# Output projection as seven quadrant products, and the stores of the residual stream ahead of fifteen expert chunks

## What is computed

```python
merged = jax.nn.sigmoid(gate_r) * y_ret + jax.nn.sigmoid(gate_m) * y_m
x = x + merged @ w_out                     # (512, 1024) @ (1024, 1024)
h = rms_norm(x, norm_ffn_w)
# router: group, then two experts of it for every token
y_e = (silu(h @ w_gate[e]) * (h @ w_up[e])) @ w_down[e]      # 32 experts, 1024 x 512 x 1024
x = x + sum over the token's two experts of weight * y_e
out = rms_norm(x, norm_final_w)
```

## Time and profile before

| | |
|---|---|
| median of three runs | 1023.38 us |
| the profiled execution | 1022.9 us |
| its span, first to last instruction | 1021.0 us |
| granted clock of TensorE, mean | 0.996 |
| TensorE matmuls, busy | 996.3 us (98%) |
| VectorE, ScalarE, GpSimd, busy | 500.1, 323.9, 120.8 us |
| moved by DMA | 269.3 MB, mean 264 GB/s |

### The profile page before, as it was taken

How to read it: one execution, slowest core, us unless ns; L and a number is a source line. 1 busy time by engine, 2 the same in 40 slices (tenths; PEclk the granted TensorE clock), 3 DMA queues, 4 the chain that set the end, 5 groups by cost and what they waited for, 6 DMA issues and landing times.

```text
span 1021.0 us, 13126 instructions
## 1 busy us (share of the span) xinstructions
PE 996.3 (98%) x4917; PEld 644.4 (63%) x4917; DVE 500.1 (49%) x810; ACT 323.9 (32%) x531; POOL 120.8 (12%) x152
## 2 busy tenths in 40 slices
PE   8999999999999999999998999999999999999896
PEld 7888788889889988888885333333333333333332
DVE  6268646597778677735525123333223233332235
ACT  6344535586556557622213100000000000000012
POOL 0683077000000000000000000000000000000000
PEclk9999999999999999999999999999999999999999
DMA  9223231344334525162988899999999999999993
GB/s 331 83 83 126 92 114 21 83 125 145 66 91 113 185 42 205 43 213 90 422 307 357 348 420 420 420 420 420 420 420 420 421 420 420 420 421 421 421 414 146
DMA packets 63125, 269.28 MB, mean 264 GB/s; under 512 B 9488, under 2 KB 9680, under 8 KB 38360
## 3 DMA queue, kind: packets, MB, share of 16 engines
q1 hardware_dynamic: 57464, 257.32, 63.6%
q0 software_dynamic: 5344, 11.02, 4.9%
q10 hardware_dynamic: 256, 0.10, 0.0%
HBM read 268.41 MB, written 4.20 MB: 267 GB/s over the span
## 4 chain that ended last, share of the span: by engine, by line
PE 72%; SPq 17%; DVE 5%; DMA 3%; ACT 2%; issue 1%; DVEq 0%; ACTq 0%
PE pj L674 23%; PE pj L854 18%; PE pj L956 12%; SPq L575 11%; PE pj L982 6%; SPq L572 6%; PE cb L631 3%; DMA raw_moe<-in_w_up_dram 3%; PE cb L992 2%; PE cb L993 1%; DVE mkT L1758 1%; DVE wl L1494 1%; PE cb L723 1%; PE cb L695 1%; ACT wh L1136 1%
## 5 line engine op out<-in xcount | busy, mean ns | idle before, releaser
L956 PE MATMUL pj<-raw_moe,xT 128*64 128x512 f32 x1016 | 227.6, 595 | 4.2 <-DMA raw_moe<-in_w_up_dram 2.4
L1494 DVE TENSOR_TENSOR wl<-raw_mix,wh 128x1024 fp32r<-128x1024 f32 x116 | 146.2, 1262 | 130.9 <-ACT wh L1136 130.6
L1970 DVE TENSOR_TENSOR x<-x,cb 128x512 f32<-128x512 f32 x120 | 77.0, 683 | 190.2 <-PE cb L993 190.2
L956 PEld LDWEIGHTS pj<-raw_moe,xT 128*64 128x64 f32 x1016 | 72.1, 137 | 140.8 <-issue 140.8
L1136 ACT ACTIVATE wh<-raw_mix 128x1024 fp32r<-128x1024 f32 x116 | 122.4, 1057 | 111.4 <-PE pj L674 68.5
L982 PE MATMUL pj<-raw_moe,hf 128*64 128x512 f32 x512 | 116.7, 598 | 1.6 <-ACT hf L1440 1.6
L982 PEld LDWEIGHTS pj<-raw_moe,hf 128*64 128x64 f32 x512 | 34.6, 136 | 67.2 <-issue 67.0
L1445 ACT ACTIVATE yh<-pj,now 128x512 fp32r<-128x512 f32 x32 | 20.4, 683 | 157.6 <-PE cb L993 143.6
L1440 ACT ACTIVATE hf<-cb 128x512 f32<-128x512 f32 x16 | 9.6, 598 | 146.3 <-PE cb L631 146.3
L992 PE MATMUL cb<-yh,hot 128*128 128x512 f32 x124 | 55.2, 445 | 0.0
L674 PE MATMUL pj<-wh,hTh 128*128 128x512 f32 x128 | 50.8, 397 | 1.7 <-DVE hTl L1525 0.7
(11 more groups left out here) (397 smaller groups left out, 1858.5 us busy)
## 6 DMA issues: line engine op xcount, KB each, us to landing
raw_moe<-in_w_gate_dram SPq DMA_DIRECT2D x64, 1024.0 KB, 26.7
raw_moe<-in_w_down_dram SPq DMA_DIRECT2D x64, 1024.0 KB, 26.7
raw_moe<-in_w_up_dram SPq DMA_DIRECT2D x63, 1024.0 KB, 26.0
raw_mix<-in_w_in_dram SPq DMA_DIRECT2D x31, 1024.0 KB, 5.3
raw_mix<-in_w_in_dram POOLq DMA_DIRECT2D x10, 512.0 KB, 5.8
raw_mix<-in_w_ret_branch_dram SPq DMA_DIRECT2D x4, 1024.0 KB, 5.8
raw_mix<-in_w_mlstm_branch_dram SPq DMA_DIRECT2D x4, 1024.0 KB, 5.5
raw_mix<-in_w_out_dram SPq DMA_DIRECT2D x4, 1024.0 KB, 5.1
```

What stands on the lines that cost most here:

```text
L956: mm = nc.tensor.matmul(pj[a * CAP:(a + 1) * CAP, up, :], xT[:, 4 * half + k, a * CAP:(a + 1) * CAP], weights_of(m + a)[:, k, :], start=ha ...
L1494: V.tensor_tensor(wl[:, q % RING, :, :], entry_source(q), wh[:, q % RING, :, :].bitcast(F32), ALU.subtract).then_inc(wl_ok, 1)
L1970: V.tensor_tensor(part, part, cb[:, 2 + g % 2, :], ALU.add).then_inc(c_add, 1)
```

## The change

The output projection is no longer two blocks but seven products of quadrants (`U_11` to `U_T4`), each in two halves `s` of 128 rows, with 14 ring entries in place of 16. The activation quadrants and their sums and differences are made by DVE (`out_part_sum`, `out_part_tail`), ACT (`out_part_head`) and POOL (`combined`, two more calls). Four quadrants of `w_out` are loaded into expert places by SP (`out_load`), three more into the ring of raw weights, and POOL issues 14 accumulating DMAs of 512 KB that make the sums of weights (`out_sums`). The results are gathered into `x2` by DVE: seven kinds of adds and subtractions of 128x512, two tiles each. Tiles 0 and 1 of `x2` are ready after the fifth product, tiles 2 and 3 after the two halves of the last one (`tile_ready`). Turning tiles 0 and 1 and the first half of the logits now stand between the products, the work on the router's weights too.

On SP only chunks 21, 13, 14, 7, 8 and 0 are left in front of the stores; the four stores follow, each behind the wait for its tile, and then fifteen chunks. Four places of `raw_moe` are exchanged. The diff, cut to its core:

```diff
-BLOCKS = 22
+BLOCKS = 20
...
-ENTRIES = 4 * (BLOCKS - 2 * len(FAST)) + FAST_ENTRIES
+OUT0 = 4 * (BLOCKS - 2 * len(FAST)) + FAST_ENTRIES
+ENTRIES = OUT0 + 2 * PRODUCTS
...
+        mrgTf = at("mrgTf", 48, [P, KD, T])
+        e5h = at("e5h", 0, [P, 4, 256], F32R)
+        e5f = at("e5f", 4, [P, 4, 256])
+        e5l = at("e5l", 24, [P, 4, 256], F32R)
+        s2h = at("s2h", 8, [P, 4, 256], F32R)
+        s2f = at("s2f", 12, [P, 4, 256])
+        s2l = at("s2l", 12, [P, 4, 256], F32R)
+        e3h = at("e3h", 16, [P, 4, 256], F32R)
+        e3f = at("e3f", 20, [P, 4, 256])
+        e3l = at("e3l", 20, [P, 4, 256], F32R)
+        t1c = at("t1c", 28, [P, 2, 512])
...
-                   enumerate([64, 72, 0, 8, 16, 24, 80, 88, 144.0625, 152.0625, 104, 120, TOP, TOP + 8, 32, 40, 48, 56, 96, 112, 194.5625, 186.0625])]
+                   enumerate([64, 72, 0, 8, 16, 24, 80, 88, 144.0625, 152.0625, 96, 112, TOP, TOP + 8, 32, 40, 48, 56, 104, 120, 194.5625, 186.0625])]
...
+        out_slot = {U_11: 12, U_T1: 13, U_T2: 0, U_T4: 1}
+        out_sums = (U_T1, U_T2, U_T2, U_T4, U_T4, U_T4, U_T3)
+        def out_place(u):
+            return raw_moe[out_slot[u]] if u in out_slot else raw_mix[slot_of(2 * B_WO + (U_T3, U_22, U_21).index(u))]
+        def out_full(u, s):
+            if u in (U_T1, U_22):
+                return tr_ps, 2 * KD + (2 if u == U_22 else 0) + s + 1
+            if u == U_21:
+                return full[2 + s], full_of(2 + s, B_WM + 1) + 1
+            return full[s], full_of(s, B_WM + 1) + (U_11, U_T2, U_T3, U_T4).index(u) + 1
+        def out_free(s, n):
+            return free[s], free_of(s, B_WM + 1) + n
+        def tile_ready(t):
+            return out_free(t % 2, 2 + t // 2 * 2)
+        def stream_bank(t, half):
+            return cb[:, 2 * t + half, :] if t < 2 else pj[:, 6 - 2 * t + half, :]
...
+            def out_load(u, c):
+                sp.dma_start(out_place(u)[:, :, :], w_out[0][0:512, 512 * c:512 * (c + 1)].rearrange("(k p) n -> p k n", p=P))\
+                    .then_inc(moe_in[out_slot[u]], 16)
+            for n in range(2 * B_WR, 2 * B_WO + 3):
+                if n == 2 * B_WR + 3:
+                    sp.wait_ge(full[1], full_fast(len(FAST) - 1, U_T2, 1))
+                    out_load(U_11, 0)
+                    out_load(U_T1, 1)
+                if n == 2 * B_WR + 4:
+                    sp.wait_ge(tr_ps, KD)
+                    out_load(U_T2, 1)
+                    out_load(U_T4, 1)
...
-            moe_chunk(13, 0, False)
-            moe_chunk(14, 0, False)
             sp.wait_ge(it_ok, 1)
             moe_chunk(21, 0, False)
-            sp.wait_ge(tr_ps, KD)
-            moe_chunk(0, 0, False)
-            moe_chunk(1, 0, False)
-            sp.wait_ge(full[3], full_of(3, B_WO - 1))
-            for m in (2, 3, 5, 6):
-                moe_chunk(m, 0, False)
-            sp.wait_ge(mgl_ok, KD)
+            sp.wait_ge(wl_ok, out_entry(U_11, 1) + 1)
+            moe_chunk(13, 0, False)
+            sp.wait_ge(wl_ok, out_entry(U_T1, 1) + 1)
+            moe_chunk(14, 0, False)
+            sp.wait_ge(mgl_ok, 7)
             moe_chunk(7, 0, False)
             moe_chunk(8, 0, False)
-            sp.wait_ge(wl_ok, ENTRIES)
-            moe_chunk(9, 0, False)
-            moe_chunk(10, 0, False)
-            sp.wait_ge(*entry_used(ENTRIES - 3))
-            for m in (11, 12, 15, 17):
-                moe_chunk(m, 0, False)
+            sp.wait_ge(wl_ok, out_entry(U_T2, 1) + 1)
+            moe_chunk(0, 0, False)
             for t in range(TT):
-                sp.wait_ge(free[t], free_of(t, BLOCKS - 1))
+                sp.wait_ge(*tile_ready(t))
                 sp.dma_start(x_dram[t * P:(t + 1) * P, :], x2[:, t, :]).then_inc(st_in, 16)
-            for m in (16, 18, 19, 20):
+            for m in (1, 2, 3, 5, 6, 9, 10, 11, 12, 15, 17, 16, 18, 19, 20):
...
-            pe.wait_ge(tr_l, 2 * KD)
-            for t in range(TT):
-                turn_stream(t)
-            pe.wait_ge(wrt_ok, 1)
-            logits(0)
+            out_parts = ((mrgTh[:, low, lower], mrgTl[:, low, lower]), (mrgTh[:, high, lower], mrgTl[:, high, lower]), (e5h, e5l), (e3h, e3l), (s2h, s2l),
+                         (mrgTh[:, low, upper], mrgTl[:, low, upper]), (mrgTh[:, high, upper], mrgTl[:, high, upper]))
+            def out_half(u, s):
+                if u == U_11:
+                    pe.wait_ge(*out_free(s, 0))
+                if u == U_21:
+                    pe.wait_ge(*out_free(2 + s, 0))
+                if u == U_22:
+                    pe.wait_ge(tr_h, 2 * KD + s + 1)
+                if u in (U_T2, U_T3, U_T4):
+                    pe.wait_ge(*out_free(s, (U_T2, U_T3, U_T4).index(u) + 1))
+                if s == 0:
+                    pe.wait_ge(mgl_ok, (1, 3, 4, 5, 6, 2, 7)[u])
+                ah, al = out_parts[u]
+                o = cb[:, s, :] if u in (U_T1, U_22) else pj[:, 2 + s, :] if u == U_21 else pj[:, s, :]
+                rows = slice(s * P, (s + 1) * P)
+                for v in range(2):
+                    q = out_entry(u, v)
+                    if s == 0:
+                        pe.wait_ge(wl_ok, q + 1)
+                    for kk in range(2):
+                        k = 2 * v + kk
+                        ops = ((ah[:, k, rows], wh[:, q % RING, kk, :]), (al[:, k, rows], wh[:, q % RING, kk, :]),
+                               (ah[:, k, rows], wl[:, q % RING, kk, :]))
+                        for n, (lhsT, rhs) in enumerate(ops):
+                            m = nc.tensor.matmul(o, lhsT, rhs, start=u in (U_11, U_21, U_T1) and k == 0 and n == 0,
+                                                 stop=k == 3 and n == 2, skip_group_check=True)
+                    if v == 1:
+                        m.then_inc(out_full(u, s)[0], 1)
+                    elif s == 1:
+                        m.then_inc(pair_used, 1)
+            for u in range(PRODUCTS):
+                for s in range(2):
+                    out_half(u, s)
+                    if u == U_T3:
+                        turn_stream(s)
+                    if u == U_T4 and s == 0:
+                        pe.wait_ge(wrt_ok, 1)
+                        logits(0)
+            turn_stream(2)
+            logit_rows(0)
+            turn_stream(3)
             logits(1)
...
+            def out_part_head(n):
+                if n in (0, 2, 6):
+                    act.wait_ge(mg_ok, 4 if n == 0 else KD)
+                if n == 0:
+                    act.wait_ge(*entry_used(entry(B_WM, 0) - 1))
+                if n in (1, 3):
+                    act.wait_ge(sum_ok, 6 * len(FAST) + (1 if n == 1 else 2))
+                if n in (4, 5):
+                    act.wait_ge(rope_ok, 2 * TT + 4 + (2 if n == 4 else 1))
+                lower, upper = slice(0, 256), slice(256, 512)
+                dst, src = ((mrgTh[:, 0:4, lower], mrg[:, 0:4, lower]), (mrgTh[:, 0:4, upper], mrgTf[:, 0:4, upper]), (mrgTh[:, 4:8, lower], mrg[:, 4:8, lower]),
+                            (e5h, e5f), (e3h, e3f), (s2h, s2f), (mrgTh[:, 4:8, upper], mrg[:, 4:8, upper]))[n]
+                nc.scalar.activation(dst[:, :, :], src[:, :, :], ACT.Copy).then_inc(mgh_ok, 1)
...
+            for x in range(2 * PRODUCTS):
+                if x == 0:
+                    out_part_head(2)
+                if x in (2 * U_T1 + 1, 2 * U_T1 + 2):
+                    out_copy(x - 2 * U_T1 - 1)
+                if OUT0 + x + LEAD < ENTRIES:
+                    mix_head(OUT0 + x + LEAD)
+                if x == 0:
+                    out_part_head(3)
+                if x in (3, 4, 5):
+                    out_part_head(x + 1)
+                if x == 2 * U_T3 + 1:
+                    square(0)
+                    stream_copy(0)
+                if x == 2 * U_T4:
+                    square(1)
+                    stream_copy(1)
...
+            def out_part_sum(n):
+                dve.wait_ge(mg_ok, 4 if n == 0 else KD)
+                lower, upper = slice(0, 256), slice(256, 512)
+                dst, one, two = ((mrgTf[:, 0:4, upper], mrg[:, 0:4, lower], mrg[:, 0:4, upper]), (e5f, mrg[:, 0:4, upper], mrg[:, 4:8, upper]))[n]
+                V.tensor_tensor(dst[:, :, :], one, two, ALU.subtract).then_inc(sum_ok, 1)
...
+                if x in (9, 10):
+                    upper_right_last(x - 9)
+                if x in (11, 12):
+                    lower_right_last(x - 11)
+                    stream_turned(x - 11)
+                if x == 13:
+                    lower_left(0)
+                if OUT0 + x + LEAD < ENTRIES:
+                    mix_tail(OUT0 + x + LEAD)
+                if x == 0:
+                    out_part_tail(2)
+                    out_part_tail(3)
+                if x in (1, 2):
+                    first_sum(x - 1)
+                if x in (3, 4):
+                    out_part_tail(x + 1)
+                if x == 5:
+                    second_sum(0)
+                    second_sum(1)
```

(35 more changed lines are left out.)

137 lines of the change are left out of this document (85 added, 52 removed).

## The result

The changed kernel takes 1052.16 us (median of four runs, 1051.13 to 1055.64) against 1022.89 for the kernel before: a ratio of 1.0291, with a 95% interval of 1.0265 to 1.0317. It is slower by 29 us, where 17 were forecast, and outside the range.

The account below looks back on a forecast made before the run. The weight stream was taken to bound the kernel: starting full 29.1 us earlier but with 19.1 MB (45.5 us) more left, +16.4 on 1022.9 gives 1039.3, plus 0.5 for the median 1039.8 us; range 1033 to 1048.

Parts of the forecast that it names:

- What bounds the kernel: Expert stage: nearly balanced, DMA the limit at the end; with weights always there it would end 3.7 us sooner.
- TensorE's saving: Output projection: 168 matmuls instead of 192, 38.1 us instead of 43.5, 5.4 us less.
- the first stall: Projection's second product: waits for the third part's tail, ready at 497.9, after the first product ends at 496.5: 1.4 us.
- DVE's release of a bank: Projection's sixth product: waits 0.3 to 1.3 us for it, 5.8 if all eight POOL operations take 1.81.
- The moved loads: SP queue: fifteen loads now behind tile 3's wait, eleven fewer under the projection; end of the stream moves by +16.4 us.
- 25 us of cover: Accumulating loads: fourteenth ends near 488, needed about 513 for the eleventh weight head; at 8 us each, 514, just late.
- two chained sums on POOL from 494.5: Projection's fourth part: 5.8 to 14.5 us of sums, 9.8 by the median, covered before its product at 508.8.
- the stalls inside the projection: TensorE's new waits in the output projection: together 1.7 to 2.7 us, bounds 0 and 7.2.
- The chain's pace: Fourteen accumulating loads of 512 KB, each after the one before landed: 6.15 us apiece, 86 us; a loaded queue 8 us.
- Rival B: Projection itself stalls: accumulate chain past 513 us, branch chunk after 467, or POOL sums late; 1047 to 1054; chance 0.13.
- The guest wait: First up product: guest chunk, last in line, lands at 580.5; TensorE stalls some 14 us, overlapping the stream's lateness.
- The branch landing beside an accumulate: Branch chunk at 454.3: up to 13 us later, at 467, if queues take turns; again just in time.

Follow-up runs that it names:

- e2: Changed kernel with the two activation sums made by DVE and none on GpSimd, accumulating loads untouched: 1041.03 us, ratio 1.0156 to 1.0250.
- e3: Kernel before, with only the order of SP's first loads changed as in the change (six, the stores, fifteen others): 1040.65 us, ratio 1.0158 to 1.0187.
- e5: e2 with each expert load issued as its place comes free, between and ahead of the stores: 1032.3 us, ratio 1.0052 to 1.0117.
- e4: Changed kernel with the guest chunk and token row issued after nine of the fifteen loads: 1054.52 us, ratio 1.0278 to 1.0329.
- e6: e2 with the guest chunk and row indices issued after nine of the fifteen loads: 1041.48 us, ratio 1.0155 to 1.0265.
- e1: Changed kernel with GpSimd's two activation sums ahead of the last two accumulating loads, not behind all fourteen: 1046.1 us, ratio 1.0208 to 1.0242.
- e12: e9 with only eight expert loads ahead of the last two stores, and the last three held until the first gather landed: 1034.33 us.
- e9: e5 with the expert loads that began at 508 held until the last accumulating load has landed: 1034.57 us, ratio 1.0091 to 1.0125.

## Why the prediction was wrong, point by point

- **What bounds the kernel: right.** The stream sets the end, with no slack late (waits of 4.0 us against 3.7), and the bytes left at 565 us give the time.
- **TensorE's saving and the first stall: right.** Without the POOL sums in the way the last store comes at 536.05 (e2), forecast 535.9. The 1.4 us in front of the second product is in the trace as 1.4. That the two agree to 0.2 us is partly luck: the 0.3 to 1.3 us for DVE's release of a bank aren't in e2's trace, and about 1 us that nobody had counted, in small gaps at the switches between products, transposes and logits, is.
- **The moved loads: right.** +16.4 forecast, +17.4 measured alone (e3).
- **"It is needed when ACT makes the eleventh weight head, about 513: 25 us of cover": the step that failed.** I looked for the chain's consumers by data, and found the weight head. Its first consumer is by queue: the activations' sums stand behind the fourteenth accumulating load in GpSimd's order, ready from 494.7. The code in the change's section shows that order; I read "two chained sums on POOL from 494.5" as if the queue were free. The cover was not 25 us but 12: at 6.15 us per load the fourteenth is issued at 482, and the sums could start at 494.7. In the forecast's sum this is the term of the stalls inside the projection: 1.7 to 2.7 us taken, 7.2 at most; the kernel after has 1.4 + 8.0, and 1.9 more for the clock behind the second.
- **The chain's pace: undersized as well.** 6.15 us were taken; from 402.17 to 506.77 the thirteen steps take 8.05 on average, the value I had as its upper bound. A landing takes about 6.4 us in most links, but 8.4 to 12.0 in five of the fourteen, and 13.1 beside eight expert loads (e5). Thirteen steps that are 1.9 us longer use up the 12 us and 13 more: the sums start at 507.5, not at 494.7. Rival B named a chain past 513 and POOL sums late as separate cases, 1047 to 1054; it was the two of them combined, at 1052, and 0.13 was too small a chance for it. (Its 524 for the chain's end at 9 us a load is a slip: fourteen of them from 402 end at 528.)
- **The sum.** The last store comes 10.0 us later than forecast. The loads' term holds: from the last store on, 203.03 MB are still to come, against the 183.93 of before from 565.04, 19.1 MB as worked out. 16.4 + 10.0 are 26.4 of the 28.8 measured. Of the other 2.4, some 1.5 are the dip of the stream from 603 to 626 us, where the prediction had no gap; the rest isn't laid to anything.
- **The guest wait: size right, role nearly right.** 12.4 us against some 14; it hides within the late stream (e4, e6), save perhaps for the dip just named. The wait of 4.6 us for the first gather, ahead of it, wasn't in the prediction; in the kernel before TensorE doesn't wait there.
- **The branch landing beside an accumulate: early enough, as the forecast took it.** ACT took the chunk at 456.57, 2.3 us later than in the earlier trace rows, and it cost nothing. What hurt was the other side, the small accumulating load beside the large ones. The Trainium skill ("DMA: Bandwidth & Descriptors", section "Queues, rings and completion order") says that engines go round the queues packet by packet, by which the landing could have come 13 us later; the trace shows 2.3, so the bound was not reached.

The range missed mainly since it treated the covers as independent of one another. I had bounded the chain by 8 us a step; with that bound and the queue's order the sums would have come out at 507, within 1 us of where they are.

## What to carry to other kernels

When work is put on an in-order queue, list everything queued behind it with the time at which it could start; the first of these is the deadline, not the consumer of the data. A stream that sets the end is measured by the bytes left at one common moment; a restart time is only a measure while the queue has run dry. Loads, stores and accumulating loads that share the DMA engines have to be placed so that the small transfer with a waiter never stands behind, or beside, bulk that has time. Work that moves to another engine is priced with its neighbour running: in e1 that cost more than the queue's order.

## What the runs showed of the hardware that was not expected

- **Sums on GpSimd and on VectorE slow each other.** The four operations of the second sum took 0.72 us each while VectorE stood idle (kernel after) and 1.70 us beside it (e1); those of the first took 1.2 us both times, but beside them VectorE's own 1024-wide subtraction took 4.47 us, against 1.22. The Trainium skill ("SBUF — State Buffer", section "Who interferes with whom") says that a VectorE instruction with two inputs in SBUF contends with GpSimd's reads; the 4.47 us and the 1.70 us agree: the subtraction reads two tiles of SBUF.
- **An accumulating load's duration depends on its neighbours.** 6.4 us for 512 KB in most links, 13.1 with eight expert loads issued while it ran (e5). With one it isn't settled: 9.4 us where the load was issued 0.8 us behind it (e12), 6.4 still where it was issued 1.9 us behind it (kernel after).
- **A store of 512 KB behind fourteen loads of its queue lands after 22.8 us** (e9), after 2.9 with none just ahead (kernel after).
- **The clock after a wait.** In the kernel after, the first 32 matmuls behind the guest wait take 9.81 us, where twice 16 take 7.3 at full clock (3.66 each); the granted clock is 0.66 on average from 580 to 600 us, a mean of its lower and its full level, after 12.4 us without a matmul.
